# Sample attention of a decoder step: key transposes between the low passes, another spacing of the key and value loads

## What is computed

```python
s = jnp.einsum('bqhd,bkhd->bhqk', qi, k, preferred_element_type=jnp.float32) * scale
s = s + fi.transpose(0, 2, 1)[..., :, None] - fk_t[..., None, :]
mask = k_pos[None, :] <= pi[:, None]
s = jnp.where(mask, s, -jnp.inf)
p = jax.nn.softmax(s, axis=-1)
return jnp.einsum('bhqk,bkhd->bqhd', p.astype(v.dtype), v)
```

## Time and profile before

| what | value |
|---|---|
| median of three runs | 3514.9 us |
| the profiled execution | 3511.37 us |
| its span, first to last instruction | 3509.6 us |
| granted TensorE clock, mean | 0.984 |
| busy share PE, DVE, ACT, POOL | 96%, 63%, 51%, 47% |
| moved by DMA | 810.17 MB, mean 231 GB/s |

### The profile page before, as it was taken

How to read it: one execution, slowest core, us unless ns; L and a number is a source line. 1 busy time by engine, 2 the same in 40 slices (tenths; PEclk the granted TensorE clock), 3 DMA queues, 4 the chain that set the end, 5 groups by cost and what they waited for, 6 DMA issues and landing times. The chain is left out here.

```text
span 3509.6 us, 54504 instructions
## 1 busy us (share of the span) xinstructions
PE 3369.2 (96%) x17111; PEld 2664.7 (76%) x17111; DVE 2194.4 (63%) x3610; ACT 1782.2 (51%) x3705; POOL 1663.9 (47%) x1239
## 2 busy tenths in 40 slices
PE   7899999999999999998999998999999998899999
PEld 6678887788787878886677676777777776778787
DVE  3425566777555556554777773888888887544432
ACT  4411222554423474645677776777777775311222
POOL 2411314153455354210688876777777777222100
PEclk9999999999999999998999999999999999999999
DMA  7878787888888887888011115999999996544422
GB/s 263 314 223 280 227 262 250 275 309 282 268 272 267 280 279 255 250 243 229 13 29 45 43 37 179 345 345 345 347 346 344 347 352 238 207 162 165 145 87 84
DMA packets 426005, 810.17 MB, mean 231 GB/s; under 512 B 97741, under 2 KB 119157, under 8 KB 425738
## 3 DMA queue, kind: packets, MB, share of 16 engines
q1 hardware_dynamic: 413650, 799.67, 68.3%
q10 hardware_dynamic: 11520, 5.12, 0.5%
q0 software_dynamic: 576, 2.10, 0.2%
HBM read 674.11 MB, written 132.67 MB: 230 GB/s over the span
## 5 line engine op out<-in xcount | busy, mean ns | idle before, releaser
L1495 PE MATMUL prj_z_ps<-prj_w_hi,prj_h_ring 128*128 128x512 f32 x1792 | 724.2, 404 | 11.1 <-DMA prj_h_ring<-hops_scratch 6.6
L1497 PE MATMUL prj_z_ps<-prj_w_hi,prj_h_ring 128*128 128x512 f32 x1792 | 703.3, 392 | 0.0
L1496 PE MATMUL prj_z_ps<-prj_w_lo,prj_h_ring 128*128 128x512 f32 x1792 | 701.6, 391 | 0.0
L1928 POOL TENSOR_TENSOR pa_p_lo<-pa_probs,pa_p_hi 128x512 fp32r<-128x512 f32 (+1 forms) x320 | 370.6, 1178 | 111.3 <-ACT pa_p_hi L1940 107.3
L1495 PEld LDWEIGHTS prj_z_ps<-prj_w_hi,prj_h_ring 128*128 128x128 f32 x1792 | 339.0, 189 | 80.8 <-issue 7.0
L2566 DVE TENSOR_TENSOR sa_kT_lo<-sa_t_ps,sa_kT_hi 128x512 fp32r<-128x512 f32 x512 | 334.1, 682 | 100.1 <-ACT sa_kT_hi L2457 97.8
L1497 PEld LDWEIGHTS prj_z_ps<-prj_w_hi,prj_h_ring 128*128 128x128 f32 x1792 | 338.2, 189 | 74.7
L1496 PEld LDWEIGHTS prj_z_ps<-prj_w_lo,prj_h_ring 128*128 128x128 f32 x1792 | 339.3, 189 | 66.6
L2436 POOL TENSOR_TENSOR sa_v_lo<-shared_v_early,sa_v_hi 128x1024 fp32r<-128x1024 f32 x130 | 310.5, 2411 | 102.1 <-DVE sa_v_hi L2572 101.8
L2436 POOL TENSOR_TENSOR sa_v_lo<-sa_v_late,sa_v_hi 128x1024 fp32r<-128x1024 f32 x126 | 301.2, 2412 | 82.1 <-DVE sa_v_hi L2572 82.0
L2457 ACT CAST sa_kT_hi<-sa_t_ps 128x512 fp32r<-128x512 f32 x512 | 278.2, 595 | 75.2 <-PE sa_t_ps L2720 69.7
(11 more groups left out here) (439 smaller groups left out, 7413.3 us busy)
## 6 DMA issues: line engine op xcount, KB each, us to landing
prj_h_ring<-hops_scratch SPq DMA_DIRECT2D x448, 512.0 KB, 4.6
arena_k_raw<-in_cache_k_dram SPq DMA_DIRECT2D x512, 256.0 KB, 4.1
shared_v_early<-in_cache_v_dram SPq DMA_DIRECT2D x260, 256.0 KB, 4.4
sa_v_late<-in_cache_v_dram SPq DMA_DIRECT2D x252, 256.0 KB, 4.4
z_scratch<-prj_z_sb SPq DMA_DIRECT2D x224, 256.0 KB, 5.5
prj_raw<-in_w_main_dram SPq DMA_DIRECT2D x104, 256.0 KB, 5.9
arena_mg<-z_scratch SPq DMA_DIRECT2D x48, 512.0 KB, 4.8
hops_scratch<-prj_h_ring SPq DMA_DIRECT2D x32, 512.0 KB, 6.1
```

Of the source, the lines that this page charges most:

```text
L1495: pe.matmul(out, h[:, 0, k], hi, start=(k == 0), stop=False)
L1496: pe.matmul(out, h[:, 0, k], lo, start=False, stop=False)
L1497: mm = pe.matmul(out, h[:, 1, k], hi, start=False, stop=(k == HK - 1))
L1928: pool.tensor_tensor(p_lo[:, s % P_RING, 0:w], probs[:, s % P_RING, 0:w], p_hi[:, s % P_RING, 0:w].bitcast(F32), ALU.subtract).then_inc(pl ...
```

## The change

1. **TensorE.** The score passes of chunk g - 1 are no longer alternated: four high ones first, then four low ones with the four transposes of page 1 of chunk g between them. The output passes likewise: the four high ones of g - 4 stand in the middle of the chunk, the four low ones at the start of the next one (chunk g - 5 there), with the four transposes of page 0 between them. Pages 2 and 3 are turned before the high output passes and after the third pass.
2. **ScalarE.** `high(g, 0)`, then in odd chunks `exp`, then `place`, `high(g, 1)`, `move`, `high(g, 2)`, the fetch of decays, `take`, `high(g, 3)`.
3. **VectorE.** In odd chunks `reduce`, `swap` and `running` stand together at the start; then `low_keys(g, 0)`, `high_values(g - 3)`, `low_keys` 1 and 2, `keep`, `low_keys` 3.
4. **Loads.** The key ring has six chunks (three in the arena, three in the shared room), the value ring four, in room that the even heads' `kA`, `qA`, `kB`, `qB` hold in the prompt's attention. Four value chunks are loaded as soon as the last even head is scored, three more key chunks where the values were loaded before. In the loop SyncE issues keys of g and then values of g - 2, and reads the page numbers of both.

```diff
-        self.v_early, = overlay(("v_early", [P, ring, CHUNK_PAGES, D_A]))
+        self.k_early, = overlay(("k_early", [P, ring, CHUNK_PAGES, D_A]))
...
+        even = one("even", [P, 4, SEQ], F32R)
+        self.even = [even[:, n] for n in range(4)]
+        self.v_ring = one("v_ring", [P, self.V_RING, CHUNK_PAGES, D_A])
...
             def begin_values():
+                sp.wait_ge(st_done, (HEADS - 1) * N_FIN)
...
+            def more_keys():
                 sp.wait_ge(turned, HEADS * TURNS)
                 sp.wait_ge(max_turned, HEADS * GROUPS)
                 sp.wait_ge(vlo_ready, 2 * HEADS)
-                v_view = cache_v.rearrange("l n k h d -> (l n) k (h d)")
...
+                    at = (arena.RING + g) * CHUNK_PAGES
+                    pages = page_numbers(nc, arena.table[0:1, bass.ds(at, CHUNK_PAGES)], k_view.shape[0])
                     for j in range(CHUNK_PAGES):
-                        src = v_view[bass.ds(pages[j], 1)].rearrange("a k x -> (a k) x")
-                        sp.dma_start(shared.v_early[:, g, j], src).then_inc(shared.v_loaded[g], 16)
+                        src = k_view[bass.ds(pages[j], 1)].rearrange("a k x -> (a k) x")
+                        sp.dma_start(shared.k_early[:, g, j], src).then_inc(shared.k_loaded[g], 16)
...
                         if g == 1:
-                            begin_values()
+                            more_keys()
...
+    RING, V_RING, BEHIND = 2 * arena.RING, Shared.V_RING, 2
...
-            def load_k(g, slot, pages):
+            def load_k(g, slot):
+                pages = find(g)
                 for j in range(CP):
                     sp.wait_ge(turned, (g - RING) * CP + (j + 1))
...
-            def load_v(w, slot, pages, first=False):
+                    page(pages[j], j, k_raw[slot], k_view, k_loaded[slot])
+
+            def load_v(w, slot):
...
+            def load_both(g, n):
+                load_k(g, n % RING)
+                load_v(g - BEHIND, (n - BEHIND) % V_RING)
+
...
                 if is_chunk(g):
                     high(g, 0)
-                    high(g, 1)
+                if odd and is_seg(s):
+                    exp(s)
...
                 if is_chunk(g - 1):
                     place(g - 1)
+                if is_chunk(g):
+                    high(g, 1)
+                if is_chunk(g - 1):
                     move(g - 1)
...
                 if is_chunk(g):
                     high(g, 2)
-                    high(g, 3)
-                if odd and is_seg(s):
-                    exp(s)
                 if is_chunk(g - 1):
                     fetch(g - 1)
                     take(g - 1)
+                if is_chunk(g):
+                    high(g, 3)
...
                 if odd and is_seg(s):
                     reduce(s)
-                if is_chunk(g):
-                    low_keys(g, 0)
-                if odd and is_seg(s):
                     swap(s)
-                if is_chunk(g):
-                    low_keys(g, 1)
+                    running(s)
+                if not odd and is_seg(s):
+                    low(s, 0)
+                    low(s, 1)
...
-                if odd and is_seg(s):
-                    running(s)
-                if not odd and is_seg(s):
-                    low(s, 0)
-                    low(s, 1)
-                    if first_seg(s):
-                        low_new(s // PER)
+                if is_chunk(g):
+                    low_keys(g, 0)
                 if is_chunk(g - 3):
                     high_values(g - 3)
...
                 if is_chunk(g):
+                    low_keys(g, 1)
                     low_keys(g, 2)
-                    low_keys(g, 3)
                 if not odd and is_seg((g - 6) // 2):
                     keep((g - 6) // 2)
+                if is_chunk(g):
+                    low_keys(g, 3)
...
+            def turn_pair(g, j, pair):
+                mm = pe.transpose(t_ps[:, j % 2, pair * PAGE:(pair + 1) * PAGE], k_raw[g % RING][:, j, pair * P:(pair + 1) * P], ident[:])
+                if pair == PAIRS - 1:
+                    mm.then_inc(turned, 1)
+
...
+                    turn_pair(g, j, pair)
+
+            def q_pair(n, pair):
+                return q_of(n)[:, pair * P:(pair + 1) * P]
+
+            def score_high(g):
+                n, slot = g // CHUNKS, g % 2
+                pe.wait_ge(khi_ready, g * CP + CP)
+                pe.wait_ge(q_placed, 4 * (n + 1))
+                wait_from(pe, taken, g - 1)
                 for pair in range(PAIRS):
-                    q = q_of(n)[:, pair * P:(pair + 1) * P]
-                    pe.matmul(out, q, hi(pair), start=(pair == 0), stop=False, skip_group_check=True)
-                    mm = pe.matmul(out[0:R], q[:, 0:R], lo(pair), start=False, stop=(pair == PAIRS - 1), skip_group_check=True)
-                return mm
...
+            def score_low_and_turn(g):
                 n, slot = g // CHUNKS, g % 2
                 pe.wait_ge(klo_ready, g * CP + CP)
-                pe.wait_ge(q_placed, 4 * (n + 1))
-                wait_from(pe, taken, g - 1)
-                score(n, s_ps[:, slot], lambda pair: kT_hi[:, slot, pair], lambda pair: kT_lo[:, slot, pair]).then_inc(scored, 1)
+                if is_chunk(g + 1):
+                    may_turn(g + 1, 1)
+                for pair in range(PAIRS):
+                    if is_chunk(g + 1):
+                        turn_pair(g + 1, 1, pair)
+                    mm = pe.matmul(s_ps[0:R, slot], q_pair(n, pair)[:, 0:R], kT_lo[:, slot, pair], start=False, stop=(pair == PAIRS - 1),
+                                   skip_group_check=True)
+                mm.then_inc(scored, 1)
...
-            def weigh(w, half):
+            def weigh_high(w):
...
-                for j in range(half * (CP // 2), (half + 1) * (CP // 2)):
+                for j in range(CP):
                     begin = slot == 0 and j == 0 and not first_seg(s)
-                    end = slot == 1 and j == CP - 1
                     pe.matmul(out, p_both[:, slot, j], v_hi[:, slot, j], start=begin, stop=False, skip_group_check=True)
-                    mm = pe.matmul(out[0:R], p_both[:, slot, j, 0:R], v_lo[:, slot, j], start=False, stop=end, skip_group_check=True)
...
+            def weigh_low_and_turn(w):
+                s, slot = divmod(w, 2)
+                g = w + WEIGH_LOW
+                for j in range(CP):
+                    if j % (CP // 2) == 0:
+                        pe.wait_ge(vlo_ready, 2 * w + j // (CP // 2) + 1)
+                    mm = pe.matmul(o_ps[0:R, s % 2], p_both[:, slot, j, 0:R], v_lo[:, slot, j], start=False, stop=(slot == 1 and j == CP - 1),
+                                   skip_group_check=True)
+                    if j == CP - 1:
+                        mm.then_inc(weighed, 1)
+                    if is_chunk(g):
+                        if j == 0:
+                            may_turn(g, 0)
+                        turn_pair(g, 0, j)
...
-            for g in range(G + 4):
+            for g in range(G + WEIGH_LOW):
                 n, c = divmod(g, CHUNKS)
                 s = (g - 3) // 2
-                if is_chunk(g):
+                if is_chunk(g - WEIGH_LOW):
+                    weigh_low_and_turn(g - WEIGH_LOW)
+                elif is_chunk(g):
                     turn(g, 0)
-                    turn(g, 1)
...
-                    first_passes(g - 1)
+                    score_high(g - 1)
+                    score_low_and_turn(g - 1)
+                elif is_chunk(g):
+                    turn(g, 1)
...
                 if is_chunk(g):
                     turn(g, 2)
-                    turn(g, 3)
                 if is_chunk(g - 4):
-                    weigh(g - 4, 0)
+                    weigh_high(g - 4)
                 if is_chunk(g - 1):
                     third_pass(g - 1)
-                if is_chunk(g - 4):
-                    weigh(g - 4, 1)
+                if is_chunk(g):
+                    turn(g, 3)
```

121 lines of the change are left out of this document (66 added, 55 removed).

## The result

The changed kernel takes 3593.2 us (median of four runs, 3587.9 to 3596.4) against 3515.5 for the kernel before, run beside it: ratio 1.0218, 95% interval 1.0200 to 1.0236, so 78 us slower. The profiled execution has a span of 3594.7 us (3509.6 before).

What follows compares the result with a forecast made beforehand. TensorE, 99% busy, was taken to bound the kernel before; the change's 12.88 us chain against 11.88 a pair costs 63 us over 63 odd chunks, less 3, so 3514.9 plus 60 gives 3575, range 3512 to 3612.

Steps and rivals of the forecast that it cites:

- the chain: Loop from an odd chunk's third pass to the next odd one's, through GpSimd and `running`: 12.88 us a pair; chance 0.72.
- the one without GpSimd: Lower bound if `running` did not wait for GpSimd: even third pass to odd one about 6.05 us, +16 to +21.
- Item 2: Low passes each beside a transpose: three times 0.34, the fourth to its end 0.40, 0.04 to the semaphore: 1.46 us.
- the 3 us that idle time should absorb: Small part of the delays between samples, expected to fall into idle time: 3 us in all, taken off 63.
- the 60: Net slowdown forecast: 63 us from the longer chain less 3 us of delays between samples, added to the median 3514.9.
- 63 pairs: The odd chunks from g = 3 on, each expected to pay 1.0 us for the longer chain: 63 us.
- TensorE's order at nothing: TensorE's new order of the same transposes and passes was taken to gain 0 us, transposes not hiding beside low passes.
- rival B: Transposes hide beside low passes on TensorE, saving 51 us; with the chain out of the way too, 3463; chance 0.04.
- Even chunks "still 5.7": Sign expected in the profile after: even chunks still take 5.7 us while pairs take 12.9.
- Rival A: The chain does not bind: `running` ends by 2.36 us in the odd chunk, waits between samples vanish, 3486 to 3491; chance 0.16.
- Rival C: Supply binds: SyncE needs over 6.45 us a chunk, or the smaller value ring pauses DMA; 3600 to 3640; chance 0.04.
- D: Nothing visible: chain and recovered waits cancel in the kernel's time, 3508 to 3522; chance 0.04.

Runs made afterwards that it cites:

- e3: Changed kernel with half of GpSimd's work left out: from the third chunk on `low_values` writes only the first half of each page's columns; 3540.0 us in one run.
- e1: Changed kernel with the exponential of odd chunks moved from ahead of `place` to behind `high` of page 2; 3576.8 us, ratio 1.0165 to the kernel before.
- e2: Changed kernel with the low output passes back in their own chunk and page 0 turned by itself, exponential still early; 3588.6 us, ratio 1.0196 to the kernel before.
- e5: Changed kernel with the exponential behind `high` 2 and `running` behind `low_keys` 0; 3576.5 us, ratio 1.0157 to the kernel before.
- e10: e5 (exponential and `running` late) with page 1's transposes put behind page 0's instead of between the low score passes; 3567.0 us, ratio 1.0144 to the kernel before.
- e6: Kernel before with only the change's loads, keeping its orders of TensorE, ScalarE and VectorE; 3517.1 us against 3520.4, ratio 1.0000.
- e4: Changed kernel with both the low output passes back in their own chunk and the exponential behind `high` 2; 3582.9 us, ratio 1.0186 to the kernel before.
- e12: e4 with page 3 turned ahead of the low output passes, third pass behind them, `high` 3 ahead of `take`, `running` behind `low_keys` 0; 3570.0 us, ratio 1.0146.
- e9: Kernel before with only bookkeeping moved: `divide` to chunk 6, output stores to chunk 7, two small sums directly behind `running`; 3527.4 us against 3515.6, ratio 1.0033.
- e11: e9 with the eight stores of a sample's output issued one in each of chunks 7 to 14; 3517.8 us against 3516.3, ratio 1.0003.

## Why the prediction was right, point by point

It said 3575, within 3512 to 3612, slower with 0.75; measured were 3593. The terms of the chain, by the changed kernel's rows above (13.16 us from third pass to third pass, 12.88 forecast):

| item | forecast | measured | rows |
|---|---|---|---|
| 1 third pass, page 3, weights | 1.11 | 1.13 | 2441.06 to 2442.19 |
| 2 low passes beside transposes | 1.46 | 1.62 | to 2443.81 |
| 3 second copy of `halves` | 0.40 | 0.41 | to 2444.22 |
| 4 `low` twice, `low_keys` 0 | 1.26 | 1.27 | to 2445.49 |
| 5 `high_values` | 1.25 | 1.29 | to 2446.78 |
| 6 GpSimd, `running` | 4.76 | 4.79 | to 2451.57 |
| 7 `exp`, `alpha` | 0.92 | 0.91 | to 2452.48 |
| 8 `place`, `high` 1, `move` | 1.72 | 1.74 | to 2454.22 |

- **The mechanism**, a loop through `halves`, `high_values`, GpSimd, `running`, `exp` and `move` that closes in every pair: right. e3 shows GpSimd in it (53 us), e1 the exponential ahead of `move` (no waits for `addend`), e2 the late low passes ahead of it (with them early `running` takes 0.22 us). But the loop is only the longest of several: cutting it in e1, e2 or e3 brought 0.35, 0.37 and 0.62 of the 1.33 us of a pair. That the sum of one loop gave the time is in part luck: had it been 0.4 to 0.6 us shorter, others would have set the time, and of these the prediction had priced the one without GpSimd too low (6.05 for the 6.28 of e3) and the bunch of e5 not at all.
- **The size.** 18 us were missing. Item 2 was short by 0.16: the passes stand 0.35 apart, not 0.34, and ScalarE's copy begins 0.57 us after the last one's start (2443.24 to 2443.81), not 0.44; a low pass beside a transpose ends 0.48 us after its start, not 0.40. With the small excesses of the others that is 0.28 x 63 = 17.6 us. Two smaller errors: a plain pair took 11.82 before, not 11.88, which I had read from a single pair (3.8 us), and the 3 us that idle time should absorb were not absorbed, 4.1 us of bookkeeping for 4.2. With the 60 these are 84.4. Against them stands a fourth: not all 63 pairs pay, since the first sample grows by 6.2 us and not by 10.5, so 4.3 us fall away. That leaves 80.1; the stage grew by 80.4 from first to last key transpose, and the medians differ by 78.
- **TensorE's order at nothing**: right for rival B, wrong beyond it. A transpose and a low pass take 0.34 to 0.35 us together, 0.11 + 0.23, so nothing hides. Even chunks without a wait take 5.77 (e2) and 5.73 (e10) where before they took 5.69; which part of the new order costs this little was not taken apart. The Trainium skill, "TensorE: Matmul & The Clock Gate", section "LDWEIGHTS (loading the stationary operand)", has a load of 128 columns take 107 ns (P/1.2 ns). If that had been the limit of a transpose, part of it would have been hidden beside the passes; the 0.34 to 0.35 us do not show it.
- **Even chunks "still 5.7"**: wrong. They took 6.08. The price that I gave TensorE's order left out what page 1's later turning does to ScalarE's and VectorE's queues (`high` 1, `move`, `high` 2, `low_keys` 2). In the change this does not lengthen the pair, for the loop's 13.15 hold it anyway, but with the loop cut it shows: with half of GpSimd's work the pair is 12.53, so 0.71 of the 1.33 us stay (e3), and 12.80 with the exponential moved besides, so 0.98 stay (e1, e5).
- **Rival A** (the chain does not bind): `running` ended 3.6 us after the odd chunk's first low output pass (2447.91 to 2451.54), not by 2.36. Even with GpSimd out of its way it ended at 3.0 (2446.15 to 2449.16 in e3), and the kernel was 19 us slower than before, not 24 to 29 faster. A left out the work of VectorE and ScalarE ahead of and behind `running`; its 0.16 was too much.
- **Rival C**: the loads are hidden, but the added addresses took 0.9 us of SyncE's queue a chunk (e6), where I had said less than 0.6 and at most 1.1 besides. **D**: no.
- **DMA**: 320 GB/s for about 325 forecast.

What is open: why a sample's bookkeeping costs 4 us in one order and 6 to 8 in others (e2, e4, e10, e12) was not taken apart. Part of it is the wait for GpSimd: with half of GpSimd's work it costs 2.3 us (102.5 - 8 x 12.53, e3). What holds the odd chunk of e4, e10 and e12 in full is open too.

## What to carry to other kernels

Follow a chain that closes on itself term by term, with the waits for a buffer to come free in it: here a copy that waited for `weighed` and a running maximum held by GpSimd set the pace of TensorE, whose wait list named neither, and the sum came within 0.3 of 13.2 us. Then ask at once what the second loop is and how far below: undoing the step that bound gave back a quarter of its cost, because other limits lay 0.35 to 0.62 us under the first, and one of them the undoing itself had raised. And when work of one engine is rearranged, look at what becomes due at the same moment on the engine that serves it; the work itself took nearly the same time here (5.73 to 5.77 for 5.69 us), and the bunch behind it cost 0.35 us in an even chunk. Last, ask of every small instruction that is moved what runs on GpSimd in its new place: the two sums gained by it, `divide` lost more.

## What the runs showed of the hardware

- A VectorE instruction with two operands in SBUF does not end before the GpSimd instruction that is running when it begins. `running` ends 0.01 to 0.03 us after it, in all 41 cases of overlap before and in 55 of 56 in the change; it takes 0.15 to 0.23 us when GpSimd is idle (before, e3, e5). The two sums took 0.73 and 0.90 before, 0.15 in e9. `divide`, 64x512, took 0.74 with GpSimd idle (e3) and 1.91 beside it (e11). The maximum over the scores and the copies of `swap`, with one such operand, were not held: 0.67 and 0.33 for two under GpSimd and beside it. The Trainium skill, "SBUF — State Buffer", section "SBUF: two separate sides", describes an exclusive lock on a port pair that VectorE and GpSimd share, held for the whole instruction and wanted by VectorE when it has two inputs in SBUF and GpSimd reads SBUF; the trace agrees.
- A pass of 512 columns with 64 columns of weights that follows a 128x128 transpose is through later than one that follows a pass: ScalarE's waiting copy begins 0.57 us after its start (2443.24 to 2443.81), against 0.43 (2405.83 to 2406.26 in the kernel before). The pace does not change: transpose and pass take 0.34 to 0.35 us, the sum of 0.11 and 0.23.
- Eight stores issued in a row hold ScalarE's queue for 2.71 us (e9).
